# Experts in two passes: U then V, with activations through DRAM, and picking and gates interleaved with U

## The chip, the cores and the metric

One core of one Trainium2 chip runs the whole program. The metric is the device time of one execution in microseconds; of the kernel before there are three runs, with a median of 5083.84 us (5082.91 to 5084.55).

## The reference

The program is two blocks over 512 tokens of width 1024, all in float32. The change touches one part of the first block, its expert layer (PEER), cut here to what matters:

```python
def chunk_fn(hc):
    q = (hc @ w_query).astype(jnp.float32).reshape(PEER_CHUNK, PEER_HEADS, PEER_DK)
    s1 = jnp.einsum('chd,hkd->chk', q[..., :PEER_HALF], keys1)
    s2 = jnp.einsum('chd,hkd->chk', q[..., PEER_HALF:], keys2)
    v1, i1 = lax.top_k(s1, PEER_TOPK)
    v2, i2 = lax.top_k(s2, PEER_TOPK)
    cand = (v1[..., :, None] + v2[..., None, :]).reshape(PEER_CHUNK, PEER_HEADS, PEER_TOPK * PEER_TOPK)
    sc, ci = lax.top_k(cand, PEER_TOPK)
    idx = (jnp.take_along_axis(i1, ci // PEER_TOPK, axis=-1) * PEER_N_KEYS
           + jnp.take_along_axis(i2, ci % PEER_TOPK, axis=-1))
    g = jax.nn.softmax(sc, axis=-1)
    act = jax.nn.gelu(jnp.einsum('chkd,cd->chk', peer_u[idx], hc), approximate=False) * g
    return jnp.einsum('chk,chkd->cd', act, peer_v[idx])
```

There are 8 heads, 128 x 128 experts, and 16 experts picked per head and token. Before it stand attention and a state space model, behind it two hybrid layers with feed-forward parts.

## The kernel before

The kernel gathers nothing. It multiplies all 512 tokens by all 16,384 rows of U, applies the Gelu, multiplies by a gate that is zero for every expert that was not picked, and multiplies the result by V. U and V are each cut into 128 weight tiles of 512 KB.

**Exact products.** A float32 operand is split into a high and a low half in the fast float32r format: ScalarE copies the raw tile (line 328, event `whi`), VectorE subtracts (line 338, event `wlo`). `three` (lines 345 to 349) then makes three matmuls of each product. One tile of U, or of the query weights, against 512 tokens is 8 x 3 = 24 matmuls of 128x512; so is one tile of V (4 token groups x 2 halves of the output x 3). Such a unit is called an item below.

**The weight stream.** All weights of the program go through one list (`Weights`). There are three raw buffers, six places for split pairs, and splits run up to four items ahead of TensorE. With item n SyncE issues the load of item n+7, since `load` (line 308) goes three beyond the splits that `reach` allows; it waits for `wlo` of item n+4, because that split frees the raw buffer. The split of n+4 waits until TensorE is done with item n-2.

**The order of the work.** Each engine has an instruction queue of its own, written out in program order; the queues meet at semaphores. The expert layer has three stages in each of them:
- Picking (`pe_pick`, `ve_pick`): 16 query items with four score matmuls each (line 1504). VectorE finds the best 16 of 128 keys by five operations (`ve_top16`), then the best 16 of 256 sums, then turns places into indices together with GpSimd (lines 1556 to 1560, 1569). TensorE fills in the 16 items of U in `PRE`, whose results are kept.
- Gates (`pe_gates` and the like): in 64 steps of 8 tokens VectorE makes one-hot matrices (lines 1651, 1652) and three bfloat16 chunks of the gate value (line 1655); TensorE multiplies them in 24 matmuls of 128x128 (line 1639), whose operands are read with a step of 8 elements; ScalarE empties the result (line 1668); it is stored to DRAM in 16 pieces of 2 MB.
- Dense (`pe_dense` and the like): in the order of `dense_order`, U items with Gelu (line 1717), the gate (line 1749) and the split into AH and AL (lines 1722, 1752), and after each four of them four V items. These four are summed in PSUM over 12 matmuls for each of 8 output tiles, and VectorE adds each to X (line 1762). Gates come back in 32 loads of 1 MB (line 1775).

Of the kernel before, what the change touches and what calls it, by code (L numbers as in the profile page):

```python
# [7 lines left out]
F = mybir.dt.float32  # L8
BF = mybir.dt.bfloat16
# [32 lines left out]
PRE = [0, 1, 2, 3] + [4 * j + 5 for j in range(12)]  # L42


def bc(ap, pos, n):
    a = ap.unsqueeze(pos)
    shape = list(a.shape)
    shape[pos] = n
    return a.broadcast_to(shape)

# [22 lines left out]
class Engine:  # L73
# [12 lines left out]
    def up(self, *event):  # L86

        return self.raised((event[0] if event else "step") + "_" + self.name, 1, event)
# [1357 lines left out]


class Peer:
    def __init__(self, k):
# [34 lines left out]
        self.O2 = [ar(128, 8, dt=BF) for _ in range(2)]
        self.RH = [ar(3, 128, 8, dt=BF) for _ in range(2)]
        k.close(2)
        ar = k.level(2 * 2048 + 1024)
        self.AH, self.AL = k.rounded("AH", 6, 512), k.rounded("AL", 6, 512)
        self.GC = [ar(16, 4, 32) for _ in range(2)]
        self.mem = ar(1024)  # L1490
        self.TT = [self.mem[:, 512 * i:512 * i + 512] for i in range(2)]
        k.close(3)

    def pe_pick(self):
        k, pe, at = self.k, self.k.pe, self.k.at
        for c in range(16):
            pe_proj(k, ("wq", c), self.XH, self.XL, 0, 4, parts=("xL", 1))
            o = k.open(4, 8, "ps", c)  # L1500
            pe.wait_ge(*at("keys"))
            pe.wait_ge(*at("pqT", c))
            for i in range(4):
                last = pe.e.matmul(o[:, 128 * i:128 * i + 128], self.QT[c % 2][:, 128 * i:128 * i + 128],
                                   self.KT[:, c, :], start=True, stop=True)
            last.then_inc(*pe.up("ps", c))
        for j in PRE:
            pe_proj(k, ("U", j), self.XH, self.XL, 0, 2)
        pe.wait_ge(*at("gg"))
# [1732 lines left out]
```

## Time and profile before

| | us |
|---|---|
| median of 3 runs | 5083.84 |
| profiled execution, whole | 5091.23 |
| its span, first to last instruction | 5089.9 |
| TensorE busy | 4432.0 (87%) |
| VectorE busy | 2518.0 (49%) |
| ScalarE busy | 1355.5 (27%) |
| GpSimd busy | 101.8 (2%) |
| DRAM read and written | 366.40 MB and 36.96 MB |

Engines are named PE (TensorE), PEld (its weight loads), DVE (VectorE), ACT (ScalarE), POOL (GpSimd) and SP (SyncE) in rows; SPq is SyncE's queue, which issues nearly all DMAs here. PEclk is the granted clock of TensorE as a share of 2.4 GHz; it is 0.50 or 1.00, and a stretch shows the mean. A matmul's duration in a row includes time that overlaps the next one, so the price of one in a stream is the distance between starts, or a stretch divided by its count.

### The profile page before, as it was taken

The page shows a single profiled execution, that of the slowest core. Times are in us where ns is not written, and L with a number is a line of the kernel's source. Part 1 is how long each engine was busy: PE and PEld are TensorE (multiplying, and loading weights), DVE is VectorE, ACT ScalarE, POOL GpSimd, SP SyncE. Part 2 cuts the span into 40 slices and gives each one's busy share as a digit, 9 for nine tenths or more (in the row PEclk, how much of TensorE's full clock was granted, in tenths as well). Part 3 has the DMA queues.
Part 4 walks back from the last instruction along what each step waited for, and adds up shares of the span by engine and source line. Part 5 has one row for each costly group of instructions (what it writes and reads, how often), then busy time and mean ns, then how long its engine had stood idle before and what let it go on. Part 6 is the DMA issues. An engine that isn't in the chain of part 4 may idle for free.

```text
span 5089.9 us, 48079 instructions
## 1 busy us (share of the span) xinstructions
PE 4432.0 (87%) x19581; PEld 3484.5 (68%) x19581; DVE 2518.0 (49%) x4268; ACT 1355.5 (27%) x2067; POOL 101.8 (2%) x75
## 2 busy tenths in 40 slices
PE   6457957998999999999899986589999998558999
PEld 6345744666888888888778764368777876436877
DVE  3764996554444444444333268643323326864331
ACT  3133211222232222222232132233223213223221
POOL 0000041000000000000000000000000000000000
PEclk8568975558999999999999987579999998768999
DMA  2001221224334333333223311012322331101332
GB/s 87 9 1 56 63 65 53 97 100 128 112 118 132 111 120 112 124 124 116 82 91 94 97 54 60 1 34 90 93 91 83 95 95 54 60 1 34 93 98 71
DMA packets 216429, 406.49 MB, mean 80 GB/s; under 512 B 11712, under 2 KB 134752, under 8 KB 214032
## 3 DMA queue, kind: packets, MB, share of 16 engines
q1 hardware_dynamic: 216208, 403.41, 25.0%
q8 instruction: 155, 2.54, 0.2%
q14 instruction: 66, 0.54, 0.0%
HBM read 366.40 MB, written 36.96 MB: 79 GB/s over the span
## 4 chain that ended last, share of the span: by engine, by line
PE 77%; DVE 17%; ACT 2%; issue 1%; DMA 1%; POOL 1%; DVEq 0%; SPq 0%; ACTq 0%; POOLq 0%
PE ps L347 21%; PE ps L348 21%; PE ps L349 21%; PE ps L1639 7%; DVE arena L1102 2%; PE ps L447 2%; DVE arena L2517 1%; PE ps L2066 1%; DVE st L2515 1%; PE ps L2042 1%; DVE arena L2434 1%; DVE arena L1419 1%; DVE wtwo L338 1%; DVE arena L1416 1%; PE ps L417 1%
## 5 line engine op out<-in xcount | busy, mean ns | idle before, releaser
L347 PE MATMUL ps<-XH,wtwo 128*128 128x512 f32 (+1 forms) x1920 | 760.3, 396 | 21.0 <-DVE wtwo L338 20.9
L338 DVE TENSOR_TENSOR wtwo<-wraw,wtwo 128x1024 fp32r<-128x1024 f32 x416 | 503.8, 1223 | 530.8 <-ACT wtwo L328 530.8
L348 PE MATMUL ps<-XL,wtwo 128*128 128x512 f32 (+1 forms) x1920 | 757.7, 395 | 0.0
L349 PE MATMUL ps<-XH,wtwo 128*128 128x512 f32 (+1 forms) x1920 | 757.1, 394 | 0.0
L328 ACT ACTIVATE wtwo<-wraw 128x1024 fp32r<-128x1024 f32 x416 | 431.3, 1050 | 601.8 <-PE ps L349 506.9
L347 PEld LDWEIGHTS ps<-XH,wtwo 128*128 128x128 f32 x1920 | 362.8, 189 | 112.5 <-issue 26.2
L349 PEld LDWEIGHTS ps<-XH,wtwo 128*128 128x128 f32 x1920 | 362.5, 189 | 87.1
L348 PEld LDWEIGHTS ps<-XL,wtwo 128*128 128x128 f32 x1920 | 362.7, 189 | 86.1
L338 DVE TENSOR_TENSOR wlast<-wraw,wlast 128x1024 fp32r<-128x1024 f32 x202 | 245.5, 1223 | 278.0 <-ACT wlast L328 278.0
L347 PE MATMUL ps<-XH,wlast 128*128 128x512 f32 x928 | 369.8, 399 | 5.1 <-DVE wlast L338 4.3
L1762 DVE TENSOR_TENSOR X<-ps,X 128x512 f32<-128x512 f32 x256 | 174.0, 689 | 403.9 <-PE ps L349 403.9
L348 PE MATMUL ps<-XL,wlast 128*128 128x512 f32 x928 | 368.2, 397 | 0.0
L349 PE MATMUL ps<-XH,wlast 128*128 128x512 f32 x928 | 368.0, 397 | 0.0
L1639 PE MATMUL ps<-arena 128*128 128x128 bf16 x1536 | 358.6, 413 | 6.8 <-DVE arena L1655 6.8
L1639 PEld LDWEIGHTS ps<-arena 128*128 128x128 bf16 x1536 | 223.5, 146 | 141.7 <-DVE arena L1655 7.2
L328 ACT ACTIVATE wlast<-wraw 128x1024 fp32r<-128x1024 f32 x202 | 210.5, 1050 | 317.7 <-PE ps L349 294.0
L347 PE MATMUL ps<-wtwo,AH 128*128 128x512 f32 x696 | 277.1, 398 | 3.0 <-DVE AL L1752 3.0
L348 PE MATMUL ps<-wtwo,AH 128*128 128x512 f32 x696 | 277.1, 398 | 0.0
L349 PE MATMUL ps<-wtwo,AL 128*128 128x512 f32 x696 | 276.9, 398 | 0.0
L347 PEld LDWEIGHTS ps<-XH,wlast 128*128 128x128 f32 x928 | 175.4, 189 | 52.3 <-issue 8.8
L349 PEld LDWEIGHTS ps<-XH,wlast 128*128 128x128 f32 x928 | 175.2, 189 | 43.0
L348 PEld LDWEIGHTS ps<-XL,wlast 128*128 128x128 f32 x928 | 175.3, 189 | 42.3
(423 smaller groups left out, 6678.1 us busy)
## 6 DMA issues: line engine op xcount, KB each, us to landing
wraw<-in_ut SPq DMA_DIRECT2D x128, 512.0 KB, 3.6
wraw<-in_v SPq DMA_DIRECT2D x128, 512.0 KB, 4.5
wraw<-in_ffn_gate SPq DMA_DIRECT2D x88, 512.0 KB, 3.5
wraw<-in_ffn_up SPq DMA_DIRECT2D x88, 512.0 KB, 3.5
wraw<-in_ffn_down SPq DMA_DIRECT2D x88, 512.0 KB, 3.5
gates<-arena SPq DMA_DIRECT2D x16, 2048.0 KB, 6.3
arena<-gates SPq DMA_DIRECT2D x32, 1024.0 KB, 6.5
wraw<-in_w_in SPq DMA_DIRECT2D x58, 512.0 KB, 3.7
```

The source lines that it names most:

```text
L328: ac.e.activation(W.items[n][7], W.rawof(n), ACT.Copy).then_inc(*ac.up("whi", n))
L338: ve.e.tensor_tensor(W.items[n][8], W.rawof(n), W.items[n][7], ALU.subtract).then_inc(*ve.up("wlo", n))
L347: mm(out, lh, rh, start=start, stop=False)
L348: mm(out, lh, rl, start=False, stop=False)
L349: return mm(out, ll, rh, start=False, stop=stop)
L417: last = k.pe.e.transpose(o[0:M, 128 * i:128 * i + 128], s, k.ident[:, :])
L447: last = pe.e.matmul(o[:, 128 * i:128 * i + 128], k.X[:, i, j * 128:(j + 1) * 128], self.D[i], start=True, stop=True)
L1102: ve.after().tensor_tensor(o, a, b, f).then_inc(*ve.up())
L1416: ve.after().max_index(idx[:, 0:8], vals[:, 0:8], src)
L1419: return ve.after().max_index(idx[:, 8:16], vals[:, 8:16], tmp)
L1639: last = pe.e.matmul(o[:, 128 * t:128 * t + 128], self.O1[n % 2][:, :, 4 * half + t], self.RH[n % 2][:, c, :, 4 * half + t], start=c == 0, ...
L1762: v.tensor_tensor(x, k.got("py", j, i, n), x, ALU.add).then_inc(*ve.free(("py", j, i, n)))
```

## The change

The three stages become two passes.

**First pass** (`pe_u`, `ve_u`, `ac_u`, `sp_u`): 16 query items and then all 128 items of U in order. `schedule` deals VectorE's picking and gate work out between them by a table of costs: about three top-16 searches an item, then the candidates, from item 63 on two gate steps an item, 64 in 32 items. TensorE's part of a gate step stands behind the following item. Index lookup is wholly VectorE's (`ve_mark`), GpSimd only makes constants. Gates are float16 in two chunks instead of bfloat16 in three, scaled by 2 to the 15, with four buffers instead of two. Each item's Gelu (256 KB) is stored to DRAM (`acts`, `sp_act`), from three buffers. The last 48 items of U have no extra work between them.

**Second pass** (`pe_v`, `ac_prep`, `ve_prep`, `sp_v`): 128 items of V, all summed in the eight banks of PSUM, added to X once at the end; the last four items are ordered by token group. Activations come back (`sp_back`, line 1757 of the changed kernel, four buffers AI), are multiplied by the gate (line 1807) and split (lines 1799, 1809), three items ahead (`LEAD`). Split lines move from 328 and 338 to 333 and 343, the load of weights from 316 to 321, gate loads from 1775 to 1749, gate matmuls from 1639 to 1563.

Semaphores of several events are merged (`SHARED`), each still raised by one engine.

```diff
-def dense_order():
-    for j in range(4):
-        yield "u", j
-    for c in range(32):
-        if c < 31:
-            yield "u", 4 * c + 4
-        yield "v", c
-        if c < 31:
-            for j in range(4 * c + 5, 4 * c + 8):
-                yield "u", j
 def plan_peer(k):
...
-    for j in PRE:
+    for j in range(128):
         W.add(("U", j), d["ut"][j], 8, 128)
-    for kind, j in dense_order():
-        if kind == "u" and j not in PRE:
-            W.add(("U", j), d["ut"][j], 8, 128)
-        if kind == "v":
-            for jj in range(4 * j, 4 * j + 4):
-                W.add(("V", jj), d["v"][:, jj, :], 1, 1024, group=("V", "of", j))
+    for j in range(128):
+        W.add(("V", j), d["v"][:, j, :], 1, 1024, group=("V", "tail") if j >= TAIL else None)
+
+TAIL = 124
...
+        self.ad = k.nc.dram_tensor("acts", (128, 128, 512), F).ap()
+        self.O1 = [ar(128, 8, dt=HF) for _ in range(4)]
+        self.RH = [ar(2, 128, 8, dt=HF) for _ in range(4)]
...
+    def schedule(self):
+        units = [("top", c, i) for c in range(16) for i in range(4)]
+        for i in range(4):
+            units += [("cand", i)] + [("best", i, h) for h in range(8)] + [("places", i)]
+            units += [("soft",)] if i == 3 else []
+            units += [("mark", i, 0), ("mark", i, 1)]
+        units += [("norm",), ("turned",)] + [("gate", n) for n in range(64)]
+        cost = {"top": 1.7, "cand": 2.5, "best": 2.4, "places": 2.5, "soft": 0.8, "mark": 7.0, "norm": 1.9,
+                "turned": 4.0, "gate": 2.8}
+        self.items = [("wq", c) for c in range(16)] + [("U", j) for j in range(128)]
+        self.units = [[] for _ in self.items]
+        self.extras = [[] for _ in range(len(self.items) + 1)]
+        time, turn = 0.0, None
+        for n, (kind, c) in enumerate(self.items):
+            time = min(time, 2.0) + (5.0 if kind == "wq" else 4.2)
+            while units and time > 0:
+                u = units[0]
+                if u[0] == "top" and n < u[1] + 2 or u[0] == "turned" and n < turn + 2:
+                    break
+                if u[0] == "gate" and sum(x[0] == "gate" for x in self.units[n]) == 2:
+                    break
+                time -= cost[u[0]]
+                if u[0] == "gate":
+                    time += 1.0
+                    self.extras[n + 1].append(u)
+                if u[0] == "norm":
+                    turn = n
+                    self.extras[n + 1].append(("turn",))
+                if u[0] == "soft":
+                    self.extras[n].append(u)
+                self.units[n].append(units.pop(0))
+        self.loads0 = max(n for n, x in enumerate(self.extras) if x) + 4
...
+    def pe_u(self):
+        k, pe, at = self.k, self.k.pe, self.k.at
+        for n, (kind, c) in enumerate(self.items):
+            if kind == "wq":
+                pe_proj(k, (kind, c), self.XH, self.XL, 0, 4, parts=("xL", 1))
+                if c:
+                    self.pe_scores(c - 1)
+            else:
+                pe_proj(k, (kind, c), self.XH, self.XL, 0, 2)
+                if c == 0:
+                    self.pe_scores(15)
+            for x in self.extras[n]:
+                if x[0] == "turn":
+                    pe.wait_ge(*at("gg"))
+                    for m, src in enumerate((self.E1, self.E2, self.GG)):
+                        pe_turn(k, [src[:, i, :, :].rearrange("p h k -> p (h k)") for i in range(4)], 128,
+                                ("peT", m), 2, 8)
+                if x[0] == "gate":
+                    self.pe_gate(x[1])
...
+    def pe_gate(self, n):
+        k, pe, at = self.k, self.k.pe, self.k.at
+        for half in range(2):
+            o = k.open(2, 8, "pg", n, half)
+            pe.wait_ge(*at("rh", n))
+            for t in range(4):
+                for c in range(2):
+                    last = pe.e.matmul(o[:, 128 * t:128 * t + 128], self.O1[n % 4][:, :, 4 * half + t],
+                                       self.RH[n % 4][:, c, :, 4 * half + t], start=c == 0, stop=c == 1)
+            last.then_inc(*pe.up("pg", n, half))
...
+    def ve_u(self):
+        k = self.k
+        does = {"top": self.ve_top, "cand": self.ve_cand, "best": self.ve_best, "places": self.ve_places,
+                "soft": self.ve_soft, "mark": self.ve_mark, "norm": self.ve_norm, "turned": self.ve_turned,
+                "gate": self.ve_gate}
+        for n, item in enumerate(self.items):
+            split_ve(k, item)
+            for u in self.units[n]:
+                does[u[0]](*u[1:])
...
+    def ve_gate(self, n):
+        k, ve, v, at = self.k, self.k.ve, self.k.ve.e, self.k.at
+        o1, o2, rh = self.O1[n % 4], self.O2[n % 4], self.RH[n % 4]
+        s = slice(8 * n, 8 * n + 8)
+        if n == 0:
+            k.begin(ve, "pick", "ve")
+        if n >= 4:
+            ve.wait_ge(*at("pg", n - 4, 1))
+        v.tensor_tensor(o2, self.IOX, bc(self.I2T[:, s], 1, 128), ALU.is_equal).then_inc(*ve.up("o2", n))
+        v.tensor_tensor(o1, self.IOX, bc(self.I1T[:, s], 1, 128), ALU.is_equal)
+        ve.wait_ge(*at("o2", n))
+        for c in range(2):
+            last = v.tensor_tensor(rh[:, c], o2, bc(self.GP[:, c, s], 1, 128), ALU.mult)
+        last.then_inc(*ve.up("rh", n))
...
+    def sp_u(self):
+        k, sp, at = self.k, self.k.sp, self.k.at
+        for n, item in enumerate(self.items):
+            load(k, item)
+            if n > 16:
+                self.sp_act(n - 17)
+            for x in self.extras[n]:
+                if x[0] == "gate" and x[1] % 4 == 3:
+                    g = x[1] // 4
+                    sp.wait_ge(*at("pgs", g))
+                    sp.e.dma_start(self.gd[g], self.GS[g % 2].rearrange("p j t -> p (j t)")).then_inc(
+                        *sp.dma(f"gstore{g % 2}", "gstore", g))
+            if n == self.loads0:
+                sp.wait_ge(*at("gstore", 14))
+                sp.wait_ge(*at("gstore", 15))
+                sp.wait_ge(*at("pg", 63, 1))
+                for c in range(2):
+                    self.sp_gc(c)
+                for j in range(3):
+                    self.sp_back(j)
+        self.sp_act(127)
...
+    def sp_act(self, j):
+        k, sp, at = self.k, self.k.sp, self.k.at
+        sp.wait_ge(*at("pact", j))
+        sp.e.dma_start(self.ad[j], self.TT[j % 3]).then_inc(*sp.dma(f"astore{j % 3}", "astore", j))
...
+    def sp_gc(self, c):
+        k, sp, at = self.k, self.k.sp, self.k.at
+        if c >= 2:
+            sp.wait_ge(*at("ag", 4 * c - 5))
+        src = self.gd[:, :, 128 * c:128 * c + 128].rearrange("g p n -> p g n")
+        sp.e.dma_start(self.GC[c % 2].rearrange("p g j t -> p g (j t)"), src).then_inc(
+            *sp.dma(f"gc{c % 2}", "gc", c))
...
+    def sp_back(self, j):
+        k, sp, at = self.k, self.k.sp, self.k.at
+        if j >= 4:
+            sp.wait_ge(*at("al", j - 4))
+        sp.wait_ge(*at("astore", j))
+        sp.e.dma_start(self.AI[j % 4], self.ad[j]).then_inc(*sp.dma(f"aback{j % 4}", "aback", j))
...
+    def pe_v(self):
+        k, pe, at = self.k, self.k.pe, self.k.at
+        ps = {(i, n): k.open(2 * i + n, 2 * i + n + 1, "py", i, n) for i in range(4) for n in range(2)}
+        def one(j, i, n, w):
+            a, c = slice(128 * i, 128 * i + 128), slice(512 * n, 512 * n + 512)
+            return three(k, ps[i, n], self.AH[:, j % 6, a], self.AL[:, j % 6, a], w[0][:, 0, c], w[1][:, 0, c],
+                         j == 0, j == 127)
+        for j in range(TAIL):
+            w = k.W.pair(("V", j))
+            pe.wait_ge(*at("wlo", w[2]))
+            pe.wait_ge(*at("al", j))
+            for i in range(4):
+                for n in range(2):
+                    last = one(j, i, n, w)
+            last.then_inc(*pe.up("pv", "V", j))
+            pe.note("wused", w[2])
+        ws = {j: k.W.pair(("V", j)) for j in range(TAIL, 128)}
+        for i in range(4):
+            for j, w in ws.items():
+                pe.wait_ge(*at("wlo", w[2]))
+                pe.wait_ge(*at("al", j))
+                for n in range(2):
+                    last = one(j, i, n, w)
+                    if j == 127:
+                        last.then_inc(*pe.up("py", i, n))
+        for j, w in ws.items():
+            pe.note("wused", w[2])
+        k.end("peer", pe)
...
+    def ac_prep(self, j):
+        k, ac, at = self.k, self.k.ac, self.k.at
+        ac.wait_ge(*at("ag", j))
+        if j >= 6:
+            ac.wait_ge(*at("pv", "V", j - 6))
+        ac.e.activation(self.AH[:, j % 6, :], self.AI[j % 4], ACT.Copy).then_inc(*ac.up("ah", j))
...
+    def ve_prep(self, j):
+        k, ve, v, at = self.k, self.k.ve, self.k.ve.e, self.k.at
+        x = self.AI[j % 4]
+        x3 = x.rearrange("p (g t) -> p g t", t=32)
+        ve.wait_ge(*at("gc", j // 4))
+        ve.wait_ge(*at("aback", j))
+        v.tensor_tensor(x3, x3, self.GC[j // 4 % 2][:, :, j % 4, :], ALU.mult).then_inc(*ve.up("ag", j))
+        ve.wait_ge(*at("ah", j))
+        v.tensor_tensor(self.AL[:, j % 6, :], x, self.AH[:, j % 6, :], ALU.subtract).then_inc(*ve.up("al", j))
...
+    def ve_v(self):
+        k, ve, v, at = self.k, self.k.ve, self.k.ve.e, self.k.at
+        for j in range(self.LEAD):
+            self.ve_prep(j)
+        for j in range(128):
+            split_ve(k, ("V", j))
+            if j + self.LEAD < 128:
+                self.ve_prep(j + self.LEAD)
+        for i in range(4):
+            for n in range(2):
+                x = k.X[:, i, 512 * n:512 * n + 512]
+                ve.wait_ge(*at("py", i, n))
+                v.tensor_tensor(x, k.got("py", i, n), x, ALU.add).then_inc(*ve.free(("py", i, n)))
+            ve.note("x+", "peer", i)
+        k.end("peer", ve)
...
+    def sp_v(self):
+        k = self.k
+        for j in range(128):
+            load(k, ("V", j))
+            if j + self.LEAD < 128:
+                self.sp_back(j + self.LEAD)
+            if j >= 5 and j % 4 == 1 and (j - 5) // 4 + 2 < 32:
+                self.sp_gc((j - 5) // 4 + 2)
```

SyncE, in the middle of the dense stage before: weights (`in_ut`, `in_v`) by fours and single gate loads; `wlo_ve` is the low half that frees a raw buffer.

```order
L316 DMA wraw<-in_v 128x1024 [waits wlo_ve] x4
L316 DMA wraw<-in_ut 128x1024 [waits wlo_ve] x2
L1775 DMA arena<-gates 128x16x128 [waits ag_ve]
L316 DMA wraw<-in_ut 128x1024 [waits wlo_ve]
L316 DMA wraw<-in_v 128x1024 [waits wlo_ve] x4
```

SyncE in the V pass of the changed kernel, its first steps; `acts` is the stored Gelu, `al_ve` the AL that frees an AI buffer.

```order
L1757 DMA arena<-acts 128x512 [waits d_astore0,al_ve]
L1749 DMA arena<-gates 128x16x128 [waits ag_ve]
L321 DMA wraw<-in_v 128x1024 [waits wlo_ve]
L1757 DMA arena<-acts 128x512 [waits d_astore1,al_ve]
L321 DMA wraw<-in_v 128x1024 [waits wlo_ve]
L1757 DMA arena<-acts 128x512 [waits d_astore2,al_ve]
L321 DMA wraw<-in_v 128x1024 [waits wlo_ve]
L1757 DMA arena<-acts 128x512 [waits d_astore0,al_ve]
L321 DMA wraw<-in_v 128x1024 [waits wlo_ve]
```

An activation's load now stands behind each weight load, and a gate load behind every fourth of these pairs.

VectorE in the dense stage before: low half of a weight, gate multiplication, AL; `free_ac` is the Gelu.

```order
L338 TENSOR_TENSOR wtwo<-wraw,wtwo 128x1024 [waits whi_ac]
L1749 TENSOR_TENSOR arena<-arena 128x512 [waits al_ve,free_ac]
L1752 TENSOR_TENSOR AL<-arena,AH 128x512 [waits ah_ac]
L338 TENSOR_TENSOR wlast<-wraw,wlast 128x1024 [waits whi_ac]
L1749 TENSOR_TENSOR arena<-arena 128x512 [waits al_ve,d_gc0,free_ac]
L1752 TENSOR_TENSOR AL<-arena,AH 128x512 [waits ah_ac]
L338 TENSOR_TENSOR wlast<-wraw,wlast 128x1024 [waits whi_ac]
L338 TENSOR_TENSOR wtwo<-wraw,wtwo 128x1024 [waits whi_ac]
L1762 TENSOR_TENSOR X<-ps,X 128x512 [waits free_ve,py_pe] x8
```

VectorE in the V pass of the changed kernel; `d_aback` is the landing of an activation, `d_gc` that of gates.

```order
L343 TENSOR_TENSOR wtwo<-wraw,wtwo 128x1024 [waits whi_ac]
L1807 TENSOR_TENSOR arena<-arena 128x512 [waits d_aback0,d_gc1]
L1809 TENSOR_TENSOR AL<-arena,AH 128x512 [waits ah_ac]
L343 TENSOR_TENSOR wtwo<-wraw,wtwo 128x1024 [waits whi_ac]
L1807 TENSOR_TENSOR arena<-arena 128x512 [waits d_aback1]
L1809 TENSOR_TENSOR AL<-arena,AH 128x512 [waits ah_ac]
L343 TENSOR_TENSOR wtwo<-wraw,wtwo 128x1024 [waits whi_ac]
L1807 TENSOR_TENSOR arena<-arena 128x512 [waits d_aback2]
L1809 TENSOR_TENSOR AL<-arena,AH 128x512 [waits ah_ac]
```

The weight's low half, the multiplication and AL still alternate. The multiplication now waits for a DMA each time, where before it waited for ScalarE and only every fourth time for a DMA.

TensorE in the gates stage before: nothing but gate matmuls, 24 a step; `rh_ve` is VectorE's right-hand operand.

```order
L1639 MATMUL ps<-arena 128x128 [waits rh_ve]
L1639 MATMUL ps<-arena 128x128 x23
L1639 MATMUL ps<-arena 128x128 [waits rh_ve,free_ac]
L1639 MATMUL ps<-arena 128x128 x11
L1639 MATMUL ps<-arena 128x128 [waits free_ac]
```

TensorE at the first gates of the changed kernel: the end of one item, two steps of 16, and the start of the next item.

```order
L352 MATMUL ps<-XH,wtwo 128x512
L353 MATMUL ps<-XL,wtwo 128x512
L354 MATMUL ps<-XH,wtwo 128x512
L1563 MATMUL ps<-arena 128x128 [waits rh_ve]
L1563 MATMUL ps<-arena 128x128 x15
L1563 MATMUL ps<-arena 128x128 [waits rh_ve]
L1563 MATMUL ps<-arena 128x128 x7
L1563 MATMUL ps<-arena 128x128 [waits free_ve]
L1563 MATMUL ps<-arena 128x128 x7
L352 MATMUL ps<-XH,wtwo 128x512 [waits wlo_ve,free_ac]
```

The 1536 gate matmuls in a row have become 32 groups of 32, each between two items of U.

## Rows read from the trace of the kernel before

**Rows 1.** The page: busy time by engine; shares of the chain that ended last.
```profile
PE 4432.0 (87%) x19581; PEld 3484.5 (68%) x19581; DVE 2518.0 (49%) x4268; ACT 1355.5 (27%) x2067; POOL 101.8 (2%) x75
...
PE 77%; DVE 17%; ACT 2%; issue 1%; DMA 1%; POOL 1%; DVEq 0%; SPq 0%; ACTq 0%; POOLq 0%
```

**Rows 2.** Busy time by stretch: length, PE, PEld, DVE, ACT, POOL, PEclk, DMA share, GB/s.
```profile
486.00:617.00 131.00, 116.73 (x547) 92.35 (x546) 111.95 (x495) 38.53 (x54) 2.73 (x4) 0.99 0.23 69
617.00:799.00 182.00, 92.33 (x370) 71.28 (x369) 171.65 (x361) 24.91 (x32) 76.31 (x35) 0.76 0.16 49
799.00:1157.00 358.00, 358.00 (x1536) 223.36 (x1536) 194.89 (x315) 76.03 (x127) 0.00 (x0) 0.50 0.21 89
1157.00:1181.00 24.00, 8.09 (x27) 6.17 (x25) 6.49 (x9) 5.77 (x8) 0.00 (x0) 0.64 0.62 196
1181.00:2526.00 1345.00, 1341.92 (x5736) 1080.26 (x5736) 622.32 (x741) 376.58 (x479) 0.00 (x0) 1.00 0.37 116
```

**Rows 3.** Timeline of PE, edges of the changed stretch: start us, us, instruction.
```profile
486.36 0.50 PE L347 MATMUL ps<-XH,wtwo 128*128 128x512 f32 x1
...
2525.52 0.40 PE L349 MATMUL ps<-wtwo,AL 128*128 128x512 f32 x1
```

**Rows 4.** Timeline of PE after the gates.
```profile
1157.03 0.79 PE L347 MATMUL ps<-XH,wlast 128*128 128x512 f32 x1
...
1161.45 0.48 PE L348 MATMUL ps<-XL,wlast 128*128 128x512 f32 x1
1161.77 0.40 PE L349 MATMUL ps<-XH,wlast 128*128 128x512 f32 x1
```

**Rows 5.** Chain that ended last, 480 to 1200 us: start us, us, what.
```profile
491.19 4.97 DMA arena<-in_keys
496.20 2.07 PE ps L1504 x8
505.15 1.17 PE ps L1504 x8
...
789.25 2.81 PE ps L417 x12
```

**Rows 6.** Line 1600, shifts beside GpSimd: duration ns min/median/max.
```profile
L1600 DVE TENSOR_SCALAR arena<-arena x4: 219/4560/4618, 652.1 to 763.0; 128x128 uint32<-128x128 uint32 x4
```

**Rows 7.** Groups by line, 799 to 1157 us (columns: see page, part 5).
```profile
L1655 DVE TENSOR_TENSOR arena<-arena 128x1024 bf16<-128x1024 bf16 x189 | 118.9, 683 | 0.0
L1668 ACT ACTIVATE arena<-ps 128x512 f32<-128x512 f32 x127 | 76.0, 599 | 292.2 <-PE ps L1639 292.2
```

**Rows 8.** Timeline of SyncE, two loads of V in a row.
```profile
1344.13 1.46 SPq L316 DMA_DIRECT2D wraw<-in_v  x2
```

**Rows 9.** Tile in_v: the time of its loads from issue to landing.
```profile
DMA to landing us min/median/max: 3.4/4.5/5.8
```

**Rows 10.** Line 1775, loads of gates, 1 MB each: the same.
```profile
DMA to landing us min/median/max: 6.1/6.5/9.2
```

**Rows 11.** DMA issues: median us from issue to landing.
```profile
arena<-skew SPq DMA_DIRECT2D x8, 256.0 KB, 4.3
...
arena<-in_keys SPq DMA_DIRECT2D x1, 1024.0 KB, 5.0
```

**Rows 12.** Timeline at the start of the dense stage.
```profile
1170.91 0.69 DVE L1749 TENSOR_TENSOR arena<-arena 128x512 f32<-128x512 f32 x1 [21.57 <-DMA arena<-gates]
1171.72 0.63 ACT L1722 ACTIVATE AH<-arena 128x512 fp32r<-128x512 f32 x1 [13.70 <-DVE arena L1749]
```

**Rows 13.** Groups by line, 1181 to 2526 us.
```profile
L338 DVE TENSOR_TENSOR wtwo<-wraw,wtwo 128x1024 fp32r<-128x1024 f32 x157 | 188.4, 1223 | 29.4 <-ACT wtwo L328 29.4
L1762 DVE TENSOR_TENSOR X<-ps,X 128x512 f32<-128x512 f32 x256 | 174.0, 689 | 403.9 <-PE ps L349 403.9
L328 ACT ACTIVATE wtwo<-wraw 128x1024 fp32r<-128x1024 f32 x157 | 160.1, 1046 | 223.8 <-PE ps L349 222.0 <-DMA wraw<-in_v 1.7
...
L1722 ACT ACTIVATE AH<-arena 128x512 fp32r<-128x512 f32 x124 | 78.4, 632 | 326.4 <-DVE arena L1749 326.4
```

More of the change, by code:

```diff
@@ L49, in bc @@
     return a.broadcast_to(shape)
+SHARED = {"statistics": ("qvar", "kvar", "aovar", "qsd", "ksd", "aosq", "aosd", "gsq", "gsd", "gss", "sqM", "xone"),
+          "operands": ("qn", "kn", "kT", "xM", "xTM", "xHM", "kv0", "SI", "dt", "mag", "gsub", "gexp", "gg")}
+SHARED = {event: name for name, events in SHARED.items() for event in events}
 class Made:
@@ L86, in up @@
     def up(self, *event):
-        return self.raised((event[0] if event else "step") + "_" + self.name, 1, event)
+        name = SHARED.get(event[0], event[0]) if event else "step"
+        return self.raised(name + "_" + self.name, 1, event)
     def raised(self, sem, n, event):
@@ L1492, in __init__ @@
         k.close(3)
-    def pe_pick(self):
-        k, pe, at = self.k, self.k.pe, self.k.at
[L1498 to L1509, printed above, removed]
-        pe.wait_ge(*at("pe2", 6))
-        for n, src in enumerate((self.E1, self.E2, self.GG)):
-            pe_turn(k, [src[:, i, :, :].rearrange("p h k -> p (h k)") for i in range(4)], 128, ("peT", n), 0, 8)
@@ new lines, in pe_scores @@
+    def pe_scores(self, c):
+        k, pe, at = self.k, self.k.pe, self.k.at
+        o = k.open(4, 8, "ps", c)
+        pe.wait_ge(*at("keys"))
+        pe.wait_ge(*at("pqT", c))
+        for i in range(4):
+            last = pe.e.matmul(o[:, 128 * i:128 * i + 128], self.QT[c % 2][:, 128 * i:128 * i + 128],
+                               self.KT[:, c, :], start=True, stop=True)
+        last.then_inc(*pe.up("ps", c))
+    def pe_gate(self, n):
[8 more added lines that the diff above has]
+            last.then_inc(*pe.up("pg", n, half))
@@ new lines, in ac_scores, with ac_gate @@
+    def ac_scores(self, c):
+        k, ac, at = self.k, self.k.ac, self.k.at
+        ac.wait_ge(*at("ps", c))
+        ac.e.activation(self.S[c].rearrange("p i k -> p (i k)"), k.got("ps", c),
+                        ACT.Copy).then_inc(*ac.free(("ps", c)))
+        ac.note("psc", c)
+    def ac_gate(self, n):
+        k, ac, at = self.k, self.k.ac, self.k.at
+        gs = self.GS[n // 4 % 2]
+        for half in range(2):
+            c0 = 8 * (n % 4) + 4 * half
+            ac.wait_ge(*at("pg", n, half))
+            if n >= 8:
+                ac.wait_ge(*at("gstore", n // 4 - 2))
+            ac.e.activation(gs[:, :, c0:c0 + 4], k.got("pg", n, half).rearrange("p (t j) -> p j t", t=4),
+                            ACT.Copy, scale=1.0 / GSCALE).then_inc(*ac.free(("pg", n, half)))
+        if n % 4 == 3:
+            ac.note("pgs", n // 4)
@@ L1627, in ve_pick @@
-        k.end("pick", ve)
-    def pe_gates(self):
-        k, pe, at = self.k, self.k.pe, self.k.at
-        for n in range(64):
-            for half in range(2):
-                o = k.open(2, 8, "pg", n, half)
-                pe.wait_ge(*at("rh", n))
-                for t in range(4):
-                    for c in range(3):
-                        last = pe.e.matmul(o[:, 128 * t:128 * t + 128], self.O1[n % 2][:, :, 4 * half + t],
-                                           self.RH[n % 2][:, c, :, 4 * half + t], start=c == 0, stop=c == 2)
-                last.then_inc(*pe.up("pg", n, half))
@@ L1793, in pe @@
     def pe(self):
         self.norm.pe()
-        self.pe_pick()
-        self.pe_gates()
-        self.k.end("gates", self.k.pe)
-        self.pe_dense()
+        self.pe_u()
+        self.k.end("u", self.k.pe)
+        self.pe_v()
     def ve(self):
@@ L1802, in ve @@
         self.norm.ve()
-        self.ve_pick()
-        self.ve_gates()
-        self.k.end("gates", self.k.ve)
-        self.ve_dense()
+        self.ve_u()
+        self.ve_v()
     def ac(self):
@@ L1810, in ac @@
         self.norm.ac()
[L1811 to L1814 removed]
+        self.ac_u()
+        self.ac_v()
     def po(self):
[L1817 to L1818 removed]
+        self.po_u()
     def sp(self):
@@ L1825, in sp @@
         sp.e.dma_start(self.KT, k.d["keys"]).then_inc(*sp.dma("keys", "keys"))
-        for c in range(16):
-            load(k, ("wq", c))
-        for j in PRE:
-            load(k, ("U", j))
-        self.sp_gates()
-        self.sp_dense()
+        self.sp_u()
+        self.sp_v()
 def plan_ffn(k, name, l):
```

340 lines of the change are left out of this document (97 added, 243 removed).

## The prediction, made before the changed kernel ran

> **What bounds the kernel now.** I read the page's shares first: TensorE is busy 87% of the span and holds 77% of the chain that ended last [rows 1]. Then a table by stretch, because the change touches only the stretch from about 486 to 2526 us [rows 2]. It shows four stages with different limits. From 486 to 617 us TensorE works at the full clock and VectorE is nearly as full. From 617 to 799 us VectorE is busy 171.65 of 182 us while TensorE stands idle half the time: picking the experts sets the end. From 799 to 1157 us (the gates, 1536 small matmuls) TensorE is busy all the time, at a granted clock of 0.50. From 1181 us on (U and V together) it is busy 1341.92 of 1345 us at 1.00. Between the last two, TensorE works 8 of 24 us: it waits for gates to go out to DRAM and come back. The edges are in single rows [rows 3]: the first projection starts at 486.36, the last V matmul at 2525.52, so it is over at 2525.9.
>
> **Unit prices.** 5736 matmuls in 1345 us [rows 2] make 0.234 us for one of 128x512; an item (one weight tile, 24 matmuls) costs 5.62. Gates: 1536 in 358 us make 0.233 for one of 128x128. At the low clock (1.2 GHz) big ones start 0.43 apart [rows 4].
>
> **First pass: queries, picking, U and gates.** Before, picking and gates stood alone; now they lie between 144 items of TensorE (16 queries, 128 U): 144 x 5.62 = 809 us. The 64 score matmuls add 64 x about 0.12 = 8 (eight take 1.17 us [rows 5]), the transposes 1. The keys land at 496.2 [rows 5]; scores are now one item later, at 497.6, so that stall goes. VectorE's picking is covered: it was busy 284 us from 486 to 799 [rows 2], some 38 of them for 31 splits; over the 62 items before the gates (348 us) it has 62 x 1.22 = 76 for splits, the old rest of 246, and the multiplications and sums that GpSimd did (14 more at 2.3 us, as long as its other operations on 2048 columns, 32), less some 20 that casts and the like lost beside a busy GpSimd (one took 0.22 to 4.6 us [rows 6]): 334. That is 96% of the cover, with four items of weights ahead; if it ran late, TensorE would wait for what is over. I take nothing. GpSimd and the third chunk of the gates are off the path.
>
> Gates: two of three chunks stay, so 64 x 16 = 1024 matmuls; at 0.233 that is 239 us. Nothing shows these at the full clock. The bound below is half, 0.117 (119 us in all), since f32 ones of 128x128 go from 0.213 (twelve in 2.81) to about 0.12 (eight in 1.17) [rows 5]; above is their own row. I take their own row, 0.233. The clock: gates held TensorE 100% busy for 358 us and it stayed at 0.50; it rose only after big matmuls followed, the first eleven of them 0.43 apart [rows 4]. Two gates, 32 matmuls, now stand between items, 32 times. If each lets the clock fall, the next item pays 11 x 0.195 = 2.1 us: 67 in all. Bounds 0 and, were all 32 items slow, 32 x 24 x 0.195 = 150. I take 67. VectorE needs 1.22 + 2 x 2.7 = 6.6 us for an item with two gates (four operations of 0.68 each) and ScalarE 1.05 + 5 x 0.6 = 4.1 [rows 7], both below TensorE's 5.62 + 7.46 = 13.1, so they hide.
>
> The Trainium skill, SBUF — State Buffer, "Door 1: The DMA port swizzle", says that each access that crosses into a new 16-byte line pays a penalty. Gate operands are read 16 bytes apart; a penalty in the memory would not shrink with the array's clock, and an item pair would cost 239 us in all; by the clock alone it would be 119. The trace agrees so far that 128x128 takes as long at 0.50 as 128x512 at 1.00, which is the same number of lines.
>
> End of U: 486.4 + 809 + 8 + 1 + 239 + 67 = 1610.
>
> **Second pass: V.** By TensorE alone it would be 128 x 5.62 = 719 us, and ScalarE (1.05 + 0.63) and VectorE (1.22 + 2 x 0.69) look idle beside it [rows 12, 13]. But the order puts a DMA into a ring. VectorE at step j writes the low half of weight j+4 (L343), then waits for activation j+3 to come back from DRAM (L1807). SyncE issues that transfer (L1757) behind the load of weight j+7 (L321), and this waits for the low half of weight j+4, the one just written. So the transfer starts when VectorE already wants it. ScalarE's next split stands behind the AH of j+3, and VectorE's next low half behind that. One round:
> SyncE, from the load's issue to the next: 1.13 us (two take 1.46, one of them ends 0.33 after its start [rows 8]).
> Landing of 256 KB: no row is the same. Loads of 512 KB land in 3.4 at the least, 4.5 in the median, queued behind each other [rows 9]; another 256 KB one takes 4.3 [rows 11]. I take 3.9, bounds 3.4 and 4.5.
> VectorE multiplies 0.69, hand-over 0.12, ScalarE's AH 0.63, its split 1.04, VectorE's split 1.22 [rows 12, 13]: 3.70. AL (0.69) lies beside the split.
> Sum 8.73 us, where TensorE needs 5.62.
> Every fourth round also waits for its 1 MB of gates, issued in the same round behind both: 2 x 1.13 + 6.5 (bounds 6.1 and 9.2 [rows 10]) + 3.70 = 12.46. Buffers would allow it earlier, the place in the queue doesn't.
> From activation 3 to 127 there are 124 rounds, 30 of them with gates: 94 x 8.73 + 30 x 12.46 = 1194. Ahead of it lie the last Gelu 0.6, the store's and the load's issue 2.3 and a landing 3.9: 6.8. Behind it 2.1 (0.69 + 0.12 + 0.63 + 0.69), then the tail: 78 matmuls still need activation 127, 78 x 0.234 = 18.3. In all 1221 us. TensorE idles in each round; a slow start after a pause costs it 2.1 and is covered by the idle time. The 248 additions into X (0.69 each) that go were beside TensorE before [rows 13] and give nothing.
>
> The Trainium skill, DMA: Bandwidth & Descriptors, "Anatomy of one DMA", fits 2.0 us plus the bytes at 436 GB/s for a transfer of the other kind of queue: 2.6 us for 256 KB and 4.4 for 1 MB. The estimate by it would be 94 x 1.3 + 30 x 2.1 = 185 us less. The trace doesn't agree for gates, 6.1 at the least, and the ring would still hold.
>
> **The sum.** V ends at 1610 + 1221 = 2831 instead of 2525.9: 305 us more; what follows is unchanged. The profiled execution took 5091.2 against a span of 5089.9, so 5396 by its own measure; the median of the runs is 7.4 lower: 5389.
>
> **The rivals.**
> Cheap gates: 1024 at 0.117 and a clock that never falls, 120 + 67 less: 5202. For it: f32 small ones do halve; between gates stand 5.6 us of full load. Against: 358 us of gates never raised the clock.
> Quick return: 256 KB alone land in 2.6 (1 MB of keys takes 5.0 [rows 11], 512 KB 3.4, so 1.6 for each 512 KB, 0.8 for 256). 94 x 1.3 = 122 less: 5267. Against it: each goes behind a load.
> No ring: should the transfer come ahead of its want, V is TensorE's, 719 + 3, 499 less: 4890, and this is the case faster than before. It needs a round under 5.62, a landing of 0.8 us; no row has that. It would need my reading of the waits to be wrong. With cheap gates too: 4703.
> Cold V: TensorE pauses 3 us and more each round; if its clock stayed at 0.50 an item would take 24 x 0.427 = 10.25, more than the mean round of 9.6, about 80 us more: 5470. Against it: back-to-back big matmuls have always brought it back [rows 4].
>
> **How the numbers follow.** Ring with dear gates 46%, cheap gates 20%, quick return 8%, cold V 11%, no ring 9%, both cheap and no ring 3%, the rest 3% slower still. The likeliest is 5389. The range 5160 to 5490 takes in cheap gates, quick return, cold V and the bounds of the landings (-47 to +56, gates -12 to +81) and leaves out the two fast cases. Faster by over 0.2% (what a measurement of this kernel tells from no change): 12% plus 2 for a mix of cheap gates and short landings: 14%. Within 0.2%: 2%. Slower: 84%.
>
> **What would show it.** In the profile after: V's stretch should last about 1220 us with TensorE busy some 60% of it; L1807 on VectorE should wait for the transfer from acts in every round and for gates in every fourth, 4 us and more; SyncE's loads of V should start 8 to 9 us apart, every fourth time 12. In U, TensorE should be busy nearly always, with items 5.6 us apart outside the gates; with them some 15 apart and a mixed clock. If V's items start 5.6 apart, the ring is wrong and with it the sign. If L1563 takes 0.117 at the full clock, the gates' term is.

## The result, and the profile after

The changed kernel takes 5331.99 us (median of 4 runs, 5329.46 to 5333.95) against 5084.19 before: a ratio of 1.0487, 95% interval 1.0469 to 1.0505. It is slower by 248 us; 305 were forecast, 5389 us. The profiled execution has a span of 5331.5 us.

The page first, busy times and then the shares of the chain that ended last. They answer to [rows 1].

```profile
PE 4470.9 (84%) x19069; PEld 3503.6 (66%) x19069; DVE 2321.0 (44%) x3968; ACT 1350.9 (25%) x2067; POOL 25.5 (0%) x40
...
PE 63%; DVE 16%; DMA 12%; ACT 5%; issue 2%; SPq 1%; POOL 0%; DVEq 0%; ACTq 0%; POOLq 0%
PE ps L352 17%; PE ps L353 17%; PE ps L354 17%; DMA arena<-acts 7%; DMA arena<-gates 5%; PE ps L1563 5%; DVE wtwo L343 2%; ACT wtwo L333 2%; DVE arena L1807 2%; DVE arena L1107 2%; PE ps L452 1%; DVE wlast L343 1%; DVE arena L2563 1%; DVE st L2561 1%; PE ps L2112 1%
```

DMA has risen from 1% of the chain to 12%. Its two lines are the loads of activations (`acts`) and of gates. The table by stretch, with the columns of [rows 2], shows where this happens:

```profile
486.00:866.00 380.00, 380.00 (x1704) 308.06 (x1704) 328.00 (x903) 114.68 (x151) 2.73 (x4) 1.00 0.44 124
866.00:1330.00 464.00, 464.00 (x1769) 325.14 (x1768) 187.04 (x279) 124.44 (x190) 0.00 (x0) 0.77 0.37 123
1330.00:1597.00 267.00, 267.00 (x1142) 214.33 (x1141) 58.60 (x48) 74.11 (x96) 0.00 (x0) 1.00 0.56 158
...
1600.00:2775.00 1175.00, 847.01 (x3072) 646.03 (x3072) 336.23 (x389) 203.91 (x261) 0.00 (x0) 0.86 0.38 112
```

In the first pass TensorE is busy all the time, so picking and gates are hidden as planned; the stretch with gates has a mixed clock. In the second it works on 3072 matmuls for 1175 us, where 719 would do. It is busy 72% of that (some 60% were forecast), since 549 of the matmuls begin at the low clock and keep it busy longer. The last U matmul starts at 1599.59 and the last of V at 2773.89, so U ends at 1600.0 and V at 2774.3, against 2525.9 before [rows 3]: the 248 us.

One round of V, in the timeline (start us, us, instruction, idle time before and what ended it):

```profile
1999.97 0.69 DVE L1807 TENSOR_TENSOR arena<-arena 128x512 f32<-128x512 f32 x1 [4.61 <-DMA arena<-acts]
2000.69 0.63 ACT L1799 ACTIVATE AH<-arena 128x512 fp32r<-128x512 f32 x1 [6.59 <-DVE arena L1807]
2001.23 1.04 ACT L333 ACTIVATE wtwo<-wraw 128x1024 fp32r<-128x1024 f32 x1
2001.36 0.69 DVE L1809 TENSOR_TENSOR AL<-arena,AH 128x512 fp32r<-128x512 f32 x1 [0.70 <-ACT AH L1799]
2002.30 1.23 DVE L343 TENSOR_TENSOR wtwo<-wraw,wtwo 128x1024 fp32r<-128x1024 f32 x1 [0.25 <-ACT wtwo L333]
2003.56 0.33 SPq L321 DMA_DIRECT2D wraw<-in_v  x1
2003.99 0.38 SPq L1757 DMA_DIRECT2D arena<-acts  x1
2008.08 0.69 DVE L1807 TENSOR_TENSOR arena<-arena 128x512 f32<-128x512 f32 x1 [4.55 <-DMA arena<-acts]
```

The reader should see the ring here. VectorE ends the weight's low half (L343) at 2003.53. SyncE issues the load it had held back 0.03 us later, and the activation's 0.43 behind that. VectorE has nothing to do until this lands, 4.1 us on. The next round begins 8.11 us after this one. What L1807 waited for in the whole pass:

```profile
  DMA arena<-acts: 433.5, 95
  DMA arena<-gates: 268.8, 30
```

### The profile page after: what moved, and what is told of

Its sections match the earlier page's. It is cut to its first block, busy times and chain, and to the rows that moved or that the text cites. A ratio compares the mean times of both kernels' runs of the same rounds, so it can differ in the third digit from the quotient of the medians.

```text
span 5331.5 us, 46851 instructions
## 1 busy us (share of the span) xinstructions
PE 4470.9 (84%) x19069; PEld 3503.6 (66%) x19069; DVE 2321.0 (44%) x3968; ACT 1350.9 (25%) x2067; POOL 25.5 (0%) x40
## 4 chain that ended last, share of the span: by engine, by line
PE 63%; DVE 16%; DMA 12%; ACT 5%; issue 2%; SPq 1%; POOL 0%; DVEq 0%; ACTq 0%; POOLq 0%
PE ps L352 17%; PE ps L353 17%; PE ps L354 17%; DMA arena<-acts 7%; DMA arena<-gates 5%; PE ps L1563 5%; DVE wtwo L343 2%; ACT wtwo L333 2%; DVE arena L1807 2%; DVE arena L1107 2%; PE ps L452 1%; DVE wlast L343 1%; DVE arena L2563 1%; DVE st L2561 1%; PE ps L2112 1%
## 5 line engine op out<-in xcount | busy, mean ns | idle before, releaser
L343 DVE TENSOR_TENSOR wtwo<-wraw,wtwo 128x1024 fp32r<-128x1024 f32 x416 | 507.7, 1224 | 871.8 <-ACT wtwo L333 871.4
L352 PE MATMUL ps<-XH,wtwo 128*128 128x512 f32 (+1 forms) x1928 | 780.8, 405 | 2.1 <-DVE wtwo L343 2.1
L354 PE MATMUL ps<-XH,wtwo 128*128 128x512 f32 (+1 forms) x1928 | 771.4, 400 | 0.0
L352 PE MATMUL ps<-wtwo,AH 128*128 128x512 f32 x688 | 310.1, 451 | 223.4 <-DVE AL L1809 223.3
L343 DVE TENSOR_TENSOR wlast<-wraw,wlast 128x1024 fp32r<-128x1024 f32 x202 | 246.7, 1224 | 445.0 <-ACT wlast L333 444.8
L352 PEld LDWEIGHTS ps<-XH,wtwo 128*128 128x128 f32 x1928 | 374.0, 194 | 95.4 <-issue 4.8
L354 PEld LDWEIGHTS ps<-XH,wtwo 128*128 128x128 f32 x1928 | 372.3, 193 | 90.5
L1807 DVE TENSOR_TENSOR arena<-arena 128x512 f32<-128x512 f32 x128 | 88.6, 692 | 702.3 <-DMA arena<-acts 433.5
L352 PEld LDWEIGHTS ps<-wtwo,AH 128*128 128x128 f32 x688 | 147.7, 215 | 290.7 <-issue 257.6
L1799 ACT ACTIVATE AH<-arena 128x512 fp32r<-128x512 f32 x128 | 80.7, 630 | 952.9 <-DVE arena L1807 952.9
L353 PE MATMUL ps<-wtwo,AH 128*128 128x512 f32 x688 | 300.1, 436 | 0.0
L354 PE MATMUL ps<-wtwo,AL 128*128 128x512 f32 x688 | 298.6, 434 | 0.0
L1563 PE MATMUL ps<-arena 128*128 128x128 f16 x1024 | 245.7, 414 | 0.0
L352 PE MATMUL ps<-wlast,AH 128*128 128x512 f32 x336 | 149.2, 444 | 103.9 <-DVE AL L1809 103.8
L1585 ACT ACTIVATE arena<-ps 128x512 f32<-128x512 f32 x128 | 76.6, 598 | 562.2 <-PE ps L354 562.2
```

Source lines behind the costliest of these rows:

```text
L343: ve.e.tensor_tensor(W.items[n][8], W.rawof(n), W.items[n][7], ALU.subtract).then_inc(*ve.up("wlo", n))
L352: mm(out, lh, rh, start=start, stop=False)
L353: mm(out, lh, rl, start=False, stop=False)
L354: return mm(out, ll, rh, start=False, stop=stop)
L1563: last = pe.e.matmul(o[:, 128 * t:128 * t + 128], self.O1[n % 4][:, :, 4 * half + t], self.RH[n % 4][:, c, :, 4 * half + t], start=c == 0, ...
L1585: a(self.TT[c % 3], k.got(("U", c)), ACT.Gelu).then_inc(*ac.free((("U", c),)))
```

## The experiments

**Half of the ring undone: the activation's load first.**

```diff
         for j in range(128):
-            load(k, ("V", j))
             if j + self.LEAD < 128:
                 self.sp_back(j + self.LEAD)
+            load(k, ("V", j))
```

> Undoes one half of the ring: SyncE issues the load of activation j+3 ahead of the load of weight j+7 instead of behind it, so it no longer waits for the low half that VectorE wrote just before; gate loads stay where they are. Ring theory: plain rounds fall from 8.02 us to TensorE's 5.62; a round with gates still takes some 12.2, and with three short ones at 3.7 (VectorE and ScalarE alone) four rounds need 23.3 us against TensorE's 22.5, so V takes 31 x 23.3 = 722 to 760 us instead of 1174 and the time is 4880 to 4920. If V were bound by the amount of DMA traffic or by a cold TensorE instead, the same bytes move and it stays above 5200.

Measured: 4908.38 us, 0.9656 of the kernel before (0.9637 to 0.9676). VectorE still waits for gates in each of the 30 rounds, but hardly for activations:

```profile
  DMA arena<-gates: 244.3, 30
  DMA arena<-acts: 37.2, 39
```

The same bytes move and TensorE's work is the same, and 424 us are gone. So traffic is out as a cause. A cold TensorE is out too: the edit doesn't touch it, and with the waits gone its clock is full by itself in the stretch of V:

```profile
1598.00:2347.00 749.00, 721.38 (x3072) 576.53 (x3072) 331.59 (x389) 204.12 (x262) 0.00 (x0) 1.00 0.58 175
```

**The other half: gates issued earlier.**

```diff
-            if j >= 5 and j % 4 == 1 and (j - 5) // 4 + 2 < 32:
-                self.sp_gc((j - 5) // 4 + 2)
+            if j % 4 == 1 and (j - 1) // 4 + 2 < 32:
+                self.sp_gc((j - 1) // 4 + 2)
```

> Undoes the other half alone: each 1 MB load of gates is issued four rounds earlier, as soon as its buffer is free; the activation's load stays behind the weight's. Ring theory: the 30 rounds of 12.52 us become rounds of 8.02, 30 x 4.5 = 135 us less: 5197. If the gate rounds cost their time through traffic that moves anyway, they only shift and the time stays at 5332.

Measured: 5209.24 us, 1.0248 (1.0228 to 1.0269), 123 less than the changed kernel, where 135 were expected. The long rounds are gone (those that issue gates now take 8.6 us); L1807 waits 125 times for an activation and never for gates:

```profile
  DMA arena<-acts: 580.6, 125
```

**Both.** The two diffs together.

> Both together: no transfer is issued behind what its own reader has just done. Ring theory: V is TensorE's alone, 128 x 5.62 = 719 and 3 us at the change of passes, 452 us less than 1174: 4880. If the clock of TensorE stays mixed in V, 30 to 100 more. If DRAM traffic (1 MB an item, 186 GB/s) binds, over 5000.

Measured: 4874.44 us, 0.9589 (0.9573 to 0.9605). The stretches with gates and of V:

```profile
862.00:1326.00 464.00, 464.00 (x1769) 325.16 (x1768) 187.63 (x280) 124.43 (x190) 0.00 (x0) 0.77 0.37 123
1598.00:2320.00 722.00, 715.69 (x3077) 579.62 (x3078) 331.69 (x392) 214.47 (x263) 0.00 (x0) 1.00 0.59 182
```

V is TensorE's now, at the full clock, with 182 GB/s moved. VectorE still waits 121.5 us for activations, but in slack that TensorE doesn't feel. So the rest of the change is worth about 210 us, and the ring cost about 458.

**More depth instead.** Four items ahead and five buffers; the order stays, and a gate load stays in the round whose activation needs it.

```diff
-        self.AI = [ar(512) for _ in range(4)]
+        self.AI = [ar(512) for _ in range(5)]
...
-    LEAD = 3
+    LEAD = 4
...
-            sp.wait_ge(*at("al", j - 4))
+            sp.wait_ge(*at("al", j - 5))
...
-            if j >= 5 and j % 4 == 1 and (j - 5) // 4 + 2 < 32:
-                self.sp_gc((j - 5) // 4 + 2)
+            if j >= 4 and j % 4 == 0 and (j - 4) // 4 + 2 < 32:
+                self.sp_gc((j - 4) // 4 + 2)
```

> The changed kernel, with activations prepared four items ahead instead of three and five buffers for them instead of four; the order on SyncE stays (an activation's load behind the weight load that waits for VectorE's last low half). Ring theory: a round still holds one landing and everything behind it, since VectorE wants the transfer as soon as it may be issued, whatever its number; 8.02 and 12.52 us a round, 5332. If it was only too little depth that showed as waiting (four buffers for a latency of 4.1 us), a fifth takes a quarter off V's rounds, down to 5040 or TensorE's bound.

Measured: 5315.42 us, 1.0464 (1.0433 to 1.0494), 17 less than the changed kernel. There is one round less, and the plain rounds take 7.95 us on average instead of 8.12. This depth doesn't open the ring, because SyncE's transfer and VectorE's use of it moved ahead together: the transfer is still issued only when it is wanted. A fifth buffer with SyncE alone one activation further ahead was not run; there the transfer would be issued a round before it is wanted.

**Two chunks alone, in the kernel before.**

```diff
-                    for c in range(3):
+                    for c in range(2):
...
-                                           self.RH[n % 2][:, c, :, 4 * half + t], start=c == 0, stop=c == 2)
+                                           self.RH[n % 2][:, c, :, 4 * half + t], start=c == 0, stop=c == 1)
```

> The kernel before with one part of the change alone: gates as two scaled float16 chunks instead of three bfloat16 ones, 1024 gate matmuls instead of 1536, all else as before. By the term of the sum: 512 x 0.233 = 119 us less than 5084: 4965. If VectorE or ScalarE came to set the pace of a gate step (2.7 and 1.2 us against TensorE's 3.7), less than that is saved; nothing in the trace says so.

Measured: 4962.03 us, 0.9762 (0.9742 to 0.9781): 121 us less. The price of a gate matmul in the sum holds, and this part alone accounts for more than half of the 210 us.

**The clock between gates.** On the version without the ring.

```diff
-                if u[0] == "gate" and sum(x[0] == "gate" for x in self.units[n]) == 2:
+                if u[0] == "gate" and any(x[0] == "gate" for x in self.units[n]):
```

> The version without the ring, with one gate step an item instead of two: 16 small matmuls (3.7 us) stand between items 64 times instead of 32 (7.5 us) 32 times. Same work. In the changed kernel the stretch with gates lasted 464 us, 50 more than 1024 x 0.234 + 31 x 5.62: the fallen clock. If it is the long group of gates that lets the clock fall, those 50 us go: 4825. If each group lets it fall whatever its length, twice as many falls cost 50 us more: 4925. If the clock has nothing to do with it, 4874.

Measured: 4874.85 us, 0.9589 (0.9573 to 0.9605), the same as without this edit. The clock was less often low, and the stretch no better:

```profile
862.00:1509.00 647.00, 647.00 (x2536) 469.99 (x2535) 226.80 (x312) 173.86 (x254) 0.00 (x0) 0.89 0.40 127
```

1024 x 0.234 + 63 x 5.62 is 594, so 53 us are still lost, spread over twice as many items. Neither of the two simple rules I had offered held. The time is that of the third, that the clock has nothing to do with it, but its reason is not: the clock did fall, and cost the same. I can't say from this what makes it fall between shorter groups.

**Dense reads, same instructions.** The changed kernel again; the gates it computes are others, as the expectation says.

```diff
-                    last = pe.e.matmul(o[:, 128 * t:128 * t + 128], self.O1[n % 4][:, :, 4 * half + t],
-                                       self.RH[n % 4][:, c, :, 4 * half + t], start=c == 0, stop=c == 1)
+                    a = 16 * (4 * half + t)
+                    last = pe.e.matmul(o[:, 128 * t:128 * t + 128], self.O1[n % 4][:, a:a + 16, :],
+                                       self.RH[n % 4][:, c, a:a + 16, :], start=c == 0, stop=c == 1)
```

> The changed kernel, in which each gate matmul reads 128 neighbouring elements of its operands instead of every eighth; it therefore computes other gates (the expert layer's result is not the reference's), while count, size and type of all instructions stay. The gate matmuls took 0.234 us at either clock, 625 of them at 1.00. If the step of 16 bytes in the read sets that, they fall to half or less, 0.117 or below: 120 us less, and with the shorter groups up to 50 more by the clock: 5165 to 5212. If the pair of weight load and matmul sets it, it stays at 0.234 and the time at 5332.

Measured: 5095.46 us, 1.0017 (1.0006 to 1.0027), 237 less than the changed kernel, more than I had thought possible. The stretch with gates:

```profile
862.00:1094.00 232.00, 232.00 (x1760) 192.64 (x1758) 187.05 (x279) 109.44 (x189) 0.00 (x0) 1.00 0.73 245
```

232 us for 31 items and 1024 gate matmuls: (232 - 174) / 1024 = 0.056 us each, a quarter of 0.234, at a clock of 1.00 from end to end. So the step of 16 bytes in the reads set the price. The edit makes both operands dense, the weights and the moving one; which of the two costs the time is not shown. Without the step the clock doesn't fall either. Whether it fell because of the reads themselves, or because they made each group four times as long (7.5 us instead of 1.8), is not separated.

**Dense reads with the right values.** No ring, one gate step an item, and VectorE writes the other layout.

```diff
-        self.RH = [ar(2, 128, 8, dt=HF) for _ in range(4)]
+        self.RH = [ar(2, 8, 128, dt=HF) for _ in range(4)]
...
-            last = v.tensor_tensor(rh[:, c], o2, bc(self.GP[:, c, s], 1, 128), ALU.mult)
+            last = v.tensor_tensor(rh[:, c], o2, bc(self.GP[:, c, s], 2, 128), ALU.mult)
```

> One gate step an item, no ring, and the one-hot matrices laid out so that TensorE's reads are dense with the right values: VectorE writes [8, 128] instead of [128, 8] and repeats its small operand along the inner dimension. If reads set the matmul's price, 1024 x 0.117 = 120 us less than the run with one gate an item, 4705 where that is 4825, provided VectorE keeps up: at 0.68 an operation it needs 3.9 us an item, at 1.2 (were the repeated operand to halve its rate) 6.0, both under TensorE's 7.5. If the pair sets the price, as the run with one gate.

Measured: 4635.71 us, 0.9117 (0.9102 to 0.9132), the best of all: 448 us under the kernel before and 239 under the run with one gate step an item, from which it differs by the layout alone. The expectation had 120 for that, again with half as the limit. As the gates are right here, other values in the operands are no explanation for the price in the run before. The stretch with gates, and VectorE's operation (duration ns min/median/max):

```profile
862.00:1276.00 414.00, 414.00 (x2535) 333.93 (x2533) 362.50 (x315) 160.01 (x255) 0.00 (x0) 1.00 0.63 198
```

```profile
L1713 DVE TENSOR_TENSOR arena<-arena x128: 1217/1219/1231, 857.8 to 1268.6; 128x1024 f16<-128x1024 f16 x128
```

VectorE pays 1.22 us an operation instead of 0.68 (they start 1.14 us apart instead of 0.60) and is busy 88% of the stretch; TensorE never waits for it.

**The same layout in the kernel before**, in its gates stage of three chunks.

> The kernel before with dense reads for its gates: VectorE writes its one-hot matrices as [8, 128], all else as before (three chunks, a stage of their own). TensorE's matmul falls from 0.233 to 0.056 us, but each of VectorE's five operations a step takes 1.22 us instead of 0.68: 6.1 us a step. In a stage of their own VectorE then sets the pace, 64 x 6.1 = 390 us against 358: 5116, slower. If TensorE's price were what counts here, 64 x 24 x 0.17 = 260 us less: 4820.

```diff
-        self.RH = [ar(3, 128, 8, dt=BF) for _ in range(2)]
+        self.RH = [ar(3, 8, 128, dt=BF) for _ in range(2)]
...
-                last = v.tensor_tensor(rh[:, c], o2, bc(self.GP[:, c, s], 1, 128), ALU.mult)
+                last = v.tensor_tensor(rh[:, c], o2, bc(self.GP[:, c, s], 2, 128), ALU.mult)
```

Measured: 5081.77 us, 1.0002 (0.9990 to 1.0013): no change. The stage went over from TensorE to VectorE:

```profile
797.00:1157.00 360.00, 160.09 (x1531) 145.10 (x1532) 357.88 (x316) 75.76 (x127) 0.00 (x0) 0.58 0.21 88
```

My 5116 was too high: five operations start 1.14 us apart, not 1.22, since neighbours overlap, so a step takes 5.7 us and not 6.1. TensorE's stage holds 63 such steps and its own last 2.7 us, 360 in all instead of 390. One step of TensorE at the low clock, as a stretch and as a row of the timeline:

```profile
803.10:805.70 2.60, 2.60 (x24) 2.40 (x24) 2.60 (x3) 0.60 (x1) 0.00 (x0) 0.50 0.00 0
803.05 2.72 PE L1639 MATMUL ps<-arena 128*128 128x128 bf16 x24 [3.02 <-DVE arena L1655]
```

That is about 0.11 us a matmul, twice the 0.056 of dense reads at the full clock. So the price of dense reads follows the clock, and that of strided ones, 0.233 or 0.234 at either, does not. The layout pays only where TensorE has other work beside it, which the interleaving of this change provides.

## Why the prediction was right

- **The ring in V** was forecast from the order alone and is what the profile shows; undoing it gives back 458 us, where the rival without a ring had put 499. V took 1174.3 us, not 1221, in three parts. The 124 rounds took 1139, not 1194. The start, from the end of U to the first round, took 12.1 instead of 6.8: on ScalarE the AH of the first three activations stand behind the last Gelu, so the low half that frees SyncE is ready only at 1607.3. The end took 23.2 instead of 20.4. The start in the changed kernel:

```profile
1600.02 0.60 ACT L1585 ACTIVATE arena<-ps 128x512 f32<-128x512 f32 x1 [4.06 <-PE ps L354]
1600.51 0.62 ACT L1799 ACTIVATE AH<-arena 128x512 fp32r<-128x512 f32 x1
1606.10 1.23 DVE L343 TENSOR_TENSOR wtwo<-wraw,wtwo 128x1024 fp32r<-128x1024 f32 x1 [0.26 <-ACT wtwo L333]
1608.03 0.32 SPq L1757 DMA_DIRECT2D arena<-acts  x1
1612.09 0.69 DVE L1807 TENSOR_TENSOR arena<-arena 128x512 f32<-128x512 f32 x1 [4.76 <-DMA arena<-acts]
```

- **The rounds.** The 94 plain rounds took 8.12 on average instead of 8.73. Landing took 4.1 (forecast 3.9) and the rest 3.6 (3.70); the miss is SyncE's term, 0.43 us from the first issue to the second and not 1.13. I had read 1.13 from two weight loads in a row [rows 8] as what an issue costs. It was a wait: the second load stood until VectorE's second low half was done at 1345.23 (two take 2.36 us from 1342.87), and went out 0.03 us later. In the kernel before:

```profile
1342.87 2.36 DVE L338 TENSOR_TENSOR wtwo<-wraw,wtwo 128x1024 fp32r<-128x1024 f32 x2 [0.26 <-ACT wtwo L328]
1345.26 0.33 SPq L316 DMA_DIRECT2D wraw<-in_v  x1
```

  The 30 rounds with gates took 12.52 (12.46), and that is luck: the two issues took 0.85 instead of 2.26, and the load of gates landed after 8.1 us instead of 6.5.
- **The first pass.** U ended at 1600.0, forecast 1610. TensorE is busy without a gap from 486 to 1597, so VectorE's picking is indeed hidden. Here too two errors cancel in part: the clock cost 17 us less than its term, and the scores cost 6 more. The program has four score matmuls a query item, but the trace records eight, and eight take the 1.17 us of [rows 5]; so there are 128 at 0.11 and not 64.
- **The price of a gate matmul** was left between 0.117 and 0.233. It is 0.234, and 625 of the 1024 began at a granted clock of 1.00, so it does not depend on the clock. The reason given with it, that the read sets it, is shown by the dense reads; what costs the time inside the memory is not. The rival of cheap gates falls.
- **The clock between gates** was put at 67 us and is 464 - 1024 x 0.234 - 31 x 5.62 = 50. The first matmuls after a group are slow, as forecast, but 8.7 on average and not eleven: between 5 and 13 of them, eight after this one:

```profile
881.08 7.68 PE L1563 MATMUL ps<-arena 128*128 128x128 f16 x32
888.40 0.79 PE L352 MATMUL ps<-XH,wtwo 128*128 128x512 f32 x1
...
891.54 0.49 PE L353 MATMUL ps<-XL,wtwo 128*128 128x512 f32 x1
891.87 0.40 PE L354 MATMUL ps<-XH,wtwo 128*128 128x512 f32 x1
```

  This is 3.47 us for what takes 1.87 at the full clock: 1.6 us an item, and with 32 items like this one 51.
- **The other rivals.** A quick return of 2.6 us did not come, 4.1 did. A cold V did not decide: the clock's mean was 0.86 there, and the slow starts lay in time in which TensorE would have waited.
- The error of 57 us is 47 from V (55 too much for the rounds, 8 too little for start and end) and 10 from the first pass.

## What to carry to other kernels

Before a transfer goes to an in-order DMA queue, ask what the instruction ahead of it waits for: here a load that waited for the reader's last step put a whole landing into every round, and swapping two lines was worth 8% of the program. One more buffer, with the reader moved ahead as far as the transfer, gave back 17 of 458 us; an earlier place in the queue gave back all. And when a small matmul costs as much at the low clock as at the full one, look at the step of its reads before anything else.

## What was not expected of the hardware

- A float16 matmul of 128x128 with operands read every 16 bytes takes 0.234 us at either clock. With dense operands it takes 0.056 at the full clock, and a bfloat16 one about 0.11 at the low clock; the four-fold gain was twice what I had set as the limit.
- With dense reads the clock stayed at 1.00 through all 1024 gate matmuls, with strided ones it fell around each of the 32 groups, and at one gate step an item the low clock still cost 53 us.
- VectorE pays for repeating an operand along its inner dimension: 1.22 us for 1024 float16 elements instead of 0.68.
- SyncE issued a load of 256 KB 0.43 us after one of 512 KB. The 1.13 us between two weight loads was no cost of the issue; it was the pace of VectorE's splits.
